# Sums of quarters on VectorE instead of GpSimd, the last projection's seven products added in PSUM, and another order of work at the entrance of the up projection

## The reference, cut to what matters

```
h2 = rms_norm(x, norm2)                      # 1024 x 1024
x  = x + square(relu(h2 @ w_up)) @ w_down    # w_up 1024 x 4096, w_down 4096 x 1024
return rms_norm(x, final_norm)
```

## Time and profile before

| what | value |
|---|---|
| median of 3 runs | 1943.54 us (1942.6 to 1944.49) |
| the profiled execution, its own time | 1942.82 us |
| its span | 1941.1 us |
| TensorE busy | 1842.5 us, 95% |
| VectorE busy | 1169.7 us, 60% |
| ScalarE busy | 918.6 us, 47% |
| GpSimd busy | 236.0 us, 12% |

### The profile page before, as it was taken

How to read it: one execution, slowest core, us unless ns; L and a number is a source line. 1 busy time by engine, 2 the same in 40 slices (tenths; PEclk the granted TensorE clock), 3 DMA queues, 4 the chain that set the end, 5 groups by cost and what they waited for, 6 DMA issues and landing times.

```text
span 1941.1 us, 23501 instructions
## 1 busy us (share of the span) xinstructions
PE 1842.5 (95%) x8913; PEld 1519.2 (78%) x8913; DVE 1169.7 (60%) x2181; ACT 918.6 (47%) x1628; POOL 236.0 (12%) x206
## 2 busy tenths in 40 slices
PE   8999999999999999999999999879999988989885
PEld 6888888868888888877888888658888867878764
DVE  5788664546676666665322244846566655576687
ACT  5566333347777777776211132335555544223222
POOL 4111001100000000000000001500000033030453
PEclk9999999999999999999999999989999989999998
DMA  5410124322232212221311143134545574443312
GB/s 168 116 33 28 55 92 147 103 65 66 61 78 70 74 54 64 76 70 60 87 49 45 54 130 119 39 103 135 168 132 176 165 277 161 153 161 131 130 66 86
DMA packets 160322, 196.41 MB, mean 101 GB/s; under 512 B 9473, under 2 KB 114505, under 8 KB 156754
## 3 DMA queue, kind: packets, MB, share of 16 engines
q1 hardware_dynamic: 154322, 182.30, 29.5%
q0 software_dynamic: 5888, 12.62, 2.9%
HBM read 139.25 MB, written 49.34 MB: 97 GB/s over the span
## 4 chain that ended last, share of the span: by engine, by line
PE 80%; DVE 12%; ACT 4%; issue 3%; POOL 0%; DMA 0%; DVEq 0%; POOLq 0%; SPq 0%; ACTq 0%
PE b L86 68%; PE b L90 8%; PE b L93 4%; DVE Xr L101 3%; DVE Wf L101 2%; DVE Wf L112 1%; ACT Wf L97 1%; DVE Yr L101 1%; DVE Wr L101 1%; ACT Wf L98 1%; DVE ringr L101 1%; ACT Xr L97 1%; DVE Wf L109 1%; ACT Wr L97 1%; DVE Yf L101 0%
## 5 line engine op out<-in xcount | busy, mean ns | idle before, releaser
L86 PE MATMUL b<-Yr,ringr 128*128 128x512 f32 x1920 | 507.9, 400 | 1.1 <-DVE Xr L101 1.1
L86 PE MATMUL b<-Xr,ringr 128*128 128x512 f32 x1584 | 394.4, 397 | 12.8 <-DVE ringr L101 9.5
L86 PEld LDWEIGHTS b<-Yr,ringr 128*128 128x128 f32 x1920 | 340.1, 189 | 56.0 <-DVE Xr L101 1.5
L86 PEld LDWEIGHTS b<-Xr,ringr 128*128 128x128 f32 x1584 | 293.7, 191 | 71.1 <-DVE ringr L101 10.8
L86 PE MATMUL b<-Xr 128*128 128x512 f32 (+3 forms) x1056 | 244.3, 373 | 13.1 <-DVE Xr L101 13.1
L86 PEld LDWEIGHTS b<-Xr 128*128 128x128 f32 x1056 | 198.8, 192 | 52.3 <-DVE Xr L101 14.7
L86 PE MATMUL b<-Yr,Xr 128*128 128x512 f32 x912 | 217.3, 397 | 16.6 <-DVE Yr L101 16.6
L86 PEld LDWEIGHTS b<-Yr,Xr 128*128 128x128 f32 x912 | 174.4, 192 | 54.3 <-DVE Yr L101 17.7
L98 ACT ACTIVATE Wf<-Wf,st 128x640 f32<-128x640 f32 (+3 forms) x192 | 125.2, 652 | 162.0 <-DVE st L116 58.8
L101 DVE TENSOR_TENSOR ringr<-stage,ringr 128x1024 fp32r<-128x1024 f32 x79 | 97.2, 1234 | 133.4 <-ACT ringr L97 133.3
L112 DVE CUSTOM_DVE_ANT_0 Wf<-b,Wf 128x256 f32<-128x256 f32 (+3 forms) x256 | 118.2, 490 | 69.8 <-PE b L86 69.2
(11 more groups left out here) (169 smaller groups left out, 2383.2 us busy)
## 6 DMA issues: line engine op xcount, KB each, us to landing
stage<-in_w_in_dram SPq DMA_DIRECT2D x58, 512.0 KB, 4.0
scratch_u<-Wf SPq DMA_DIRECT2D x80, 256.0 KB, 3.8
Wf<-scratch_u SPq DMA_DIRECT2D x14, 1024.0 KB, 4.8
stage<-scratch_u SPq DMA_DIRECT2D x13, 1024.0 KB, 4.8
stage<-in_w_up_dram SPq DMA_DIRECT2D x24, 512.0 KB, 4.3
stage<-in_w_out_dram SPq DMA_DIRECT2D x16, 512.0 KB, 3.5
scratch_x<-Wf SPq DMA_DIRECT2D x16, 512.0 KB, 2.7
Xr<-Xr POOLq DMA_DIRECT2D x32, 256.0 KB, 3.3
```

Of the source, the lines that this page charges most:

```text
L86: return self.send(lambda e: e.matmul(o, w, a, start=start, stop=stop))
```

## The change

It does three things.

1. **Work of GpSimd goes to VectorE.** T3 of the row tiles 4 to 6, T4 of all row tiles (`T4f` in the list) and the four sums of quarters of each strip (`quarter_sum`) become VectorE instructions. GpSimd keeps only `rstd`.
2. **Products are added in PSUM.** In the last projection P1, P6, P7 and P4 use one set of four banks and P5, P3 and P2 the other. P6 is added by TensorE onto the bank in which P1 stands, P7 onto that, P4 onto that; P3 onto P5. So each eviction goes straight into a quarter of the result (c11, c12, c22, c21) and the running sums and their joining fall away. The residual x2 is loaded beside and added by four VectorE instructions of 128x2048 in the third strip (`add_x2`). DOWN_ORDER changes.
3. **The entrance gets another order**, room_a22 two buffers, and "P3" is split into "P3" and "C12" in the list.

```diff
-DOWN_ORDER = ("P1", "P5", "P7", "P6", "P3", "P2", "P4")
+DOWN_ORDER = ("P1", "P5", "P6", "P3", "P7", "P2", "P4")
-LAST_BANKS = (6, 4, 5, 1, 7, 2, 3, 0)
+DOWN_BANKS, OTHER_DOWN_BANKS = (6, 4, 5, 1), (7, 2, 3, 0)
...
-            b = LAST_BANKS[(4 * n + t) % 8]
+            b = (DOWN_BANKS if kind in ("P1", "P6", "P7", "P4") else OTHER_DOWN_BANKS)[t]
             pe.wait_ge(*at[freed[b]])
...
+                    if kind in ("P1", "P2", "P5"):
+                        sent = pe.matmul(m.banks[b], own, other, k == 0 and i == 0, k == 3 and i == 2)
+                    else:
+                        sent = pe.matmul_onto(m.banks[b], own, other, k == 3 and i == 2)
...
-    out = [("post", 7), ("a", 1), ("lows", 6), ("row", 7), ("s12f", 0), ("P1", 0), ("T3", 6), ("P2", 0), ("C11", 0),
-           ("tile", 7), ("P1", 1), ("T3", 7), ("P2", 1), ("s43f", 0), ("s43", 0), ("P5", 0), ("a22", 0),
-           ("P6", 0), ("s12f", 1), ("P3", 0), ("s12", 1), ("P7", 0), ("s43f", 1), ("US", 0), ("C11", 1), ("P5", 1), ("s43", 1),
-           ("T4", 4), ("P6", 1), ("T4", 5), ("T4", 6), ("T4", 7), ("P4", 0), ("U4", 0), ("a", 2), ("P3", 1), ("P1", 2),
-           ("s12f", 2), ("a22", 1), ("P7", 1), ("s12", 2)]
+    out = [("post", 7), ("lows", 6), ("T3", 6), ("row", 7), ("s12f", 0), ("P1", 0), ("P2", 0), ("C11", 0), ("P1", 1),
+           ("s12", 0), ("tile", 7), ("s43f", 0), ("P2", 1), ("T3", 7), ("s43", 0), ("P5", 0), ("a22", 0), ("P6", 0),
+           ("s12f", 1), ("P3", 0), ("C12", 0), ("s12", 1), ("P7", 0), ("s43f", 1), ("P5", 1), ("s43", 1), ("US", 0),
+           ("C11", 1), ("a22", 1), ("P6", 1), ("a", 2), ("P3", 1), ("C12", 1), ("T4f", 4), ("P1", 2), ("s12f", 2),
+           ("P7", 1), ("T4", 4), ("s12", 2), ("T4f", 5), ("P5", 2), ("T4", 5), ("s43f", 2), ("T4f", 6), ("P2", 2),
+           ("s43", 2), ("T4", 6), ("T4f", 7), ("P6", 2), ("T4", 7), ("a", 3), ("P3", 2), ("s12f", 3), ("P4", 0),
+           ("U4", 0), ("US", 1), ("C12", 2), ("C11", 2), ("s12", 3), ("P4", 1), ("U4", 1), ("a22", 2)]
...
-            out += [("prepS", 0), ("P6", i), ("a22", i), ("P3", i), ("prepT", 0), ("P7", i), ("US", i), ("P4", i),
-                    ("U4", i)]
+            out += [("prepS", 0), ("P6", i), ("a22", i), ("P3", i), ("C12", i), ("P7", i), ("prepT", 0), ("US", i),
+                    ("P4", i), ("U4", i)]
...
-    quarter = {"P1": m.sum1, "P5": m.sum5, "P6": m.sum6, "P7": m.sum7, "P2": m.c11, "P3": m.c12, "P4": m.c21}
+    quarter = {"P1": m.c11, "P2": m.c11, "P6": m.c12, "P3": m.c12, "P5": m.c22, "P7": m.c22, "P4": m.c21}
...
     for n in range(28):
-        added(n, 0)
+        c, x = n // 7, n % 7
         if n == 27:
             row_out(3)
+        added(n, 0)
         if n + 1 < 28:
             prep_low(n + 1, "S")
+        if n == 0:
+            quarter_sum("T1", 0)
         added(n, 1)
...
+        if x in (0, 2, 4):
+            quarter_sum({0: "T2", 2: "T3", 4: "T4"}[x], c)
+        elif x == 6 and c < 3:
+            quarter_sum("T1", c + 1)
+        elif c == 2 and x in (1, 3, 5):
+            add_x2({1: "P5", 3: "P6", 5: "P1"}[x], n)
+        elif n == 8:
+            add_x2("P4", 6)
```

More of the change, by code:

```diff
@@ L1645, in scalar_program @@
             relu_square("A12", i, m.ua12, m.banks[p], ("P4", i), ("kept", "A12", i - 1) if i else ("turned", "f", 7, 1))
[L1646 removed]
+        elif kind in ("a", "s12", "s43", "a22"):
             weights_high(kind, i)
@@ L1672, in scalar_program @@
         for t in range(4):
-            if c == 0 and kind in sums:
+            if c == 0 and kind in first:
                 act.wait_ge(*at["back", n, t])
@@ L1676, in scalar_program @@
                     act.wait_ge(*at["P4", PAIRS - 1])
[L1677 to L1678 removed]
+                    for name in STORED:
+                        act.wait_ge(*at["kept", name, PAIRS - 1])
+                act.activation(first[kind][:, t, :], m.banks[note.bank["back", n, t]], FN.Copy).then_inc(
                     m.a_ev, ("added", n, t))
[L1680 to L1683 removed]
+            elif c == 3 and kind in ("P3", "P7", "P2", "P4"):
                 act.wait_ge(*at["added", n, t])
[L1685 to L1692 removed]
+                last_square(t if kind in ("P3", "P2") else 4 + t, int(kind in ("P3", "P7")))
 def back_source(m, c, kind):
@@ L2396, in added @@
         dve.wait_ge(*at["back", n, t])
-        if c == 0:
-            dve.wait_ge(*at[f"x2 for {kind}"])
-        else:
-            dve.wait_ge(*at["added", n - 7, t])
-        if c == 3 and kind == "P2":
-            dve.wait_ge(*at["C11 with P1"])
-        elif c == 3 and kind == "P3":
-            dve.wait_ge(*at["C12 with P5"])
-        elif c == 3 and kind == "P6":
-            dve.wait_ge(*at["P6 with P1"])
-        elif c == 3 and kind == "P4":
-            dve.wait_ge(*at["C21 with P7"])
@@ L2409, in added @@
-        dve.tensor_tensor(dst, dst, m.banks[note.bank["back", n, t]], ALU.add).then_inc(m.v_ev, ("added", n, t))
-        if c == 3 and kind == "P3":
-            dve.wait_ge(*at["added", n, t])
-            dve.wait_ge(*at["added", n - 1, t])
-            dve.tensor_tensor(m.c12[:, t, :], m.c12[:, t, :], m.sum6[:, t, :], ALU.add).then_inc(
-                m.v_ev, ("C12 whole", t))
+        dve.wait_ge(*at[{"P1": ("added", n - 2, t), "P2": ("added", n - 5, t), "P6": ("added", n - 6, t),
+                         "P3": ("added", n - 1, t), "P5": ("added", n - 4, t), "P7": ("added", n - 3, t),
+                         "P4": ("added", n - 7, t)}[kind]])
@@ new lines, in added, with add_x2 @@
+        if (kind, c) in (("P1", 3), ("P5", 3), ("P6", 3), ("P4", 3)):
+            dve.wait_ge(*at["x2 added", kind])
+        dve.tensor_tensor(dst, dst, m.banks[note.bank["back", n, t]], ALU.add).then_inc(m.v_ev, ("added", n, t))
+    def add_x2(kind, n):
+        dst, x = quarter[kind], ("P1", "P5", "P6", "P4").index(kind)
+        dve.wait_ge(*at["x2 again", kind])
+        for t in range(4):
+            dve.wait_ge(*at["added", n, t])
+        dve.tensor_tensor(dst, dst, m.x2_quarter[x], ALU.add).then_inc(m.v_ev, ("x2 added", kind))
@@ L2642, in gpsimd_program @@
-    pool.wait_ge(*at["P7 with P6"])
-    pool.wait_ge(*at["added", 20, 3])
-    onto(m.c21, m.sum7, "C21 with P7")
-    rstd("end", 4, 0)
-    pool.wait_ge(*at["C22 with P5"])
-    onto(m.c22, m.sum7, "C22 whole")
-    for t in range(1, NT):
-        rstd("end", 4, t)
+    for stage, slot in (("f", 3), ("end", 4)):
+        for t in range(NT):
+            rstd(stage, slot, t)
 def sync_program(sp, m, at, note, units, swa, att):
```

241 lines of the change are left out of this document (96 added, 145 removed).

## The result

| | before | after |
|---|---|---|
| median | 1943.07 us (1940.5 to 1944.49, 4 runs) | 1893.45 us (1893.22 to 1897.08, 4 runs) |
| ratio of after to before | | 0.975, 95% interval 0.9734 to 0.9767 |
| profiled execution, own time | 1942.82 us | 1893.29 us |
| its span | 1941.1 us | 1890.9 us |

The change makes the kernel faster by 49.6 us; predicted were 51.9, from 1943.54 to 1891.6. The page after, to be held against the earlier trace rows: TensorE has as many instructions as before and 13.4 us less busy time, GpSimd 91.7 us instead of 236.0.

The account below looks back on a forecast made before the run. TensorE, busy for 95% of the span, was taken as the bound, with only its waits and slow running to win. -41.7 - 6.9 - 4.4 + 1.1 = -51.9 gave 1890.9, as median 1891.6 us; own range 1887 to 1897, wider 1884 to 1904.

Parts of the forecast that it names:

- Last projection: The last 28 products: without GpSimd's additions TensorE no longer waits, 305.4 us instead of 347.1, -41.7 us.
- the walk: The prediction's stepping through the engines' queues by instruction durations; in the last projection it left a margin of 2.4 us.
- Turn: Between up projection and last projection: product 0 starts at 1572.2 instead of 1579.1, -6.9 us.
- End: Behind the last matmul: without joining sums holding back rows, 10.5 us instead of 14.9, -4.4 us.
- Entrance: The kernel's first stage: 22.7 us of TensorE waits plus slow running, 31.8 lost against 30.6, +1.1 in the sum.
- The third: Rival: VectorE becomes the bound in the last projection, +14 (1905 us) or at the far bound +38 (1930); chance 0.11.
- the first: Rival: the entrance gets better as well, with shorter TensorE waits, some -8, 1883 us; chance 0.14.
- second: Rival: the entrance gets worse than walked, one late step passed through all three queues, +8 to +10, 1900 us; chance 0.10.
- The fifth: Rival: in the last projection GpSimd's adds have little to do with the waits, about 1935 to 1943 us; chance 0.02.
- The fourth: Rival: TensorE, gapless for 305 us, partly gets its lower clock level; slower than before, 1947.5 us and more; chance 0.02.
- the advice that the prediction cites: Trainium skill: work may move off a saturated VectorE, even to GpSimd; by it the third rival's 1905 us would result.

Follow-up runs that it names:

- experiments 7 and 8: The changed kernel with unneeded GpSimd additions of 128x2048 beside products 4 and 11: pairs in 7 (1903.14 us), single ones in 8 (1897.13 us).
- Experiment 5: The changed kernel with two unneeded GpSimd additions of 128x2048 beside each of products 2, 4 and 6: 1899.02 us.
- experiment 6: The changed kernel with six GpSimd memsets, which write SBUF and read none, beside each of products 2, 4 and 6: 1893.01 us.
- experiment 3: The kernel before with only the 16 sums of quarters moved from GpSimd to VectorE, nothing added in PSUM: 1921.44 us.
- experiment 4: The changed kernel with the sums of quarters back on GpSimd, the adding in PSUM kept: 1905.21 us.
- experiment 2: The kernel before with the new order of entrance and turn, and T3 and T4 on VectorE, but the old last projection: 1942.39 us.
- experiment 1: The kernel before with the new last projection and end alone; entrance, turn, and T3 and T4 on GpSimd as before: 1896.59 us.

## Why the prediction was right

**Last projection (-41.7; measured -40.7).** The mechanism was that of VectorE's additions beside GpSimd's. The prediction told it of the low halves alone and counted seven waits for them; two of these, 0.93 and 6.77 us, have low halves of 2.28 and 2.29 us, and the last comes from stretched joining adds (experiments 7 and 8). The change removes both kinds, so the number did not suffer. Experiment 5 shows it with work that nobody needs, experiment 6 that only reading does it, and experiments 7 and 8 put the slack where the walk had it, 2.4 us. The choice of 2.29 us for a sum was right, and none of the 27 products behind product 0 waits. The 1.0 us that is missing is in product 0: from its start to product 1's are 12.6 us, not 10.9, as it runs slowly behind its wait of 2.37. I had put 0.8 us on the whole for this.

**What of it is the sums, and what the adding in PSUM.** The prediction took both in one term and did not divide it. The runs do: the sums alone bring 20 us (experiment 3), the PSUM adding with the sums left on GpSimd, and the new order, 36 (experiment 4), all together 49.6. They overlap, since both take additions away from GpSimd, and a product whose two low halves are hit waits far more than twice as long as one with a single hit (5.0 against 1.3 us).

**Turn (-6.9; -6.8).** P4's wait was forecast at 0.8 and is 0.87, product 0 at 1572.2 and starts at 1572.87, of which 0.6 is the entrance's. It needs both parts of the change: the order alone gives the wait to product 0 (experiment 2), the silent GpSimd alone leaves 4.80 us at P4 (experiment 1). GpSimd need not be wholly silent, though: in experiment 4 the sum T1 runs on it from 1569.76 to 1574.37, is done before the low half begins at 1575.12, and the two waits are 0.87 and 2.37 us as in the changed kernel. What hit product 0 in experiment 2 was the sum that followed at once.

**End (-4.4; -3.3).** This term was mis-sized by 1.1 us. VectorE ends 9.0 us behind the last product, not 7.8. These are the scalings of rows 5 to 7 on it:

```profile
1881.55 1.41 DVE L109 SCALAR_TENSOR_TENSOR Wf<-Wf,ssq,stage 128x512 f32<-128x512 f32 x2 [0.66 <-POOL ssq L101]
...
1884.48 1.41 DVE L109 SCALAR_TENSOR_TENSOR Wf<-Wf,ssq,stage 128x512 f32<-128x512 f32 x2 [0.66 <-POOL ssq L101]
...
1886.82 1.41 DVE L109 SCALAR_TENSOR_TENSOR Wf<-Wf,ssq,stage 128x512 f32<-128x512 f32 x2 [0.66 <-POOL ssq L101]
```

The last product ends at 1879.26. Row 5 is done at 1881.55 + 1.41, 3.7 us behind that, where the walk had 2.9; rows 6 and 7 then take 2.3 us each beside the last addition's 0.6, where it had 2.15: 0.8 + 0.2 + 0.2 = 1.2. The pitch of 2.34 us stood in the earlier trace rows; the walk used 2.15 to 2.2. It fits rows 0 to 3, which are 2.2 apart beside the adds, and not rows 4 to 7; 0.3 us more come ahead of row 4, where VectorE waits 0.19 us for ScalarE.

**Entrance (+1.1; +0.6).** Seven waits came as walked, within 0.4 us, and an eighth of 0.18 came beside them. Forecast and measured: 4.7 and 4.61, 1.6 and 1.60, 4.6 and 4.22, 4.9 and 4.83, 0.7 and 0.76, 1.1 and 0.87, 5.1 and 4.68:

```profile
1249.18 4.37 PE L86 MATMUL b<-Xr,ringr 128*128 128x512 f32 x12 [4.61 <-DVE Xr L101]
...
1269.23 3.04 PE L90 MATMUL b<-Xr,Yr 128*128 128x512 f32 x12 [0.18 <-DVE Yr L101]
...
1276.49 4.35 PE L86 MATMUL b<-Xr,Wr 128*128 128x512 f32 x12 [4.22 <-DVE Wr L101]
...
1319.55 7.71 PE L86 MATMUL b<-Xr,ringr 128*128 128x512 f32 x24 [4.68 <-DVE ringr L101]
```

The store that P5 of pair 3 hangs on is there as walked. VectorE's two evictions wait 3.43 us for it, where the walk had 3.8:

```profile
1314.10 1.29 DVE L101 TENSOR_TENSOR Wf<-Wf,b 128x512 f32<-128x512 f32 x2 [3.43 <-DMA scratch_u<-Wf]
```

Part of the hit is luck. The terms given for that product add up to 13.7 us and not to 13.3, which would make its wait 5.5 and not 5.1; and 22.7 us of waits with four times 2.2 of slow running are 31.5, not 31.8. Measured are 21.7 us of waits and, of 31.2 lost, 9.5 of slow running: the first was put 1.0 too high, the second some 0.4 to 0.7 too low.

**The rivals.** The third (VectorE becomes the bound) fell with the sum at 2.29 us; the first and second (another entrance) with the waits above. The fifth (it does not do what it says) fell in experiments 3 and 5. The fourth, a lower level of the clock in 300 us without a gap, did not come: the granted clock was 1.00 there. Moving GpSimd's work onto a busier engine was right here: giving the sums back to GpSimd makes the last projection 9.2 us longer (experiment 4). The first half of the advice that the prediction cites is for a saturated VectorE, and this one was busy for 60% of the span.

## What to carry to other kernels

A VectorE addition of 128x2048 with both inputs in SBUF that starts while a GpSimd addition runs costs its own 2.3 us plus what is left of the other's. Ask what the lateness of a product's operands adds up to, and how much slack it meets: a single stretched low half cost 0.9 us and two in a row 5.8 (experiments 8 and 7), so measure the slack before pricing a move. And where all the waits of a stretch come from an order written by hand while no engine is full there, walk the queues: TensorE's waits could be foretold to about 0.4 us from durations alone, in part by luck, and rewriting the list brought another 18 us, 7 of them the slow running that follows long waits.
